# One projection piece of the fourth group moves from the eighth to the ninth step of the first attention branch, and the group's evacuation from the ninth to the tenth

## The reference, cut to what matters

```python
h = rmsnorm(x)
a_q, a_k, a_v, b_q, b_k, b_v, c_q, c_k, c_v, c_f, gates = split(h @ w_in)
# A, 4 heads, two maps each of width 64, values of width 128, keys up to the query's chunk of 64:
p = softmax(q k / 8 + t5 bias);  o_a = (p[map 0] - lam * p[map 1]) @ v, then a norm
# B, 8 heads: a band of 9 chunks; C, 8 heads: causal with a forget bias
x = x + (g0 * (o_a @ w_br_a) + g1 * (o_b @ w_br_b) + g2 * (o_c @ w_br_c)) @ w_out
x = x + (silu(h2 @ w_gate) * (h2 @ w_up)) @ w_down
out = rmsnorm(x)
```

## Time and profile before

| | us |
|---|---|
| median of 3 runs | 1947.63 |
| lowest, highest | 1944.6, 1948.3 |
| the profiled execution's own time | 1945.05 |
| its span | 1943.0 |
| PE busy | 1884.4 (97%) |
| DVE busy | 1150.8 (59%) |
| ACT busy | 815.8 (42%) |
| mean granted PE clock | 0.991 |

### The profile page before, as it was taken

The page is one execution under the profiler, slowest core; times in us unless marked ns, Lnnn a source line. Parts: engine busy times, 40 slices in busy tenths (PEclk is TensorE's granted clock), DMA queues, the critical chain, the costliest instruction groups (busy, mean ns, idle before and its releaser), DMA issues. The chain is left out here.

```text
span 1943.0 us, 27344 instructions
## 1 busy us (share of the span) xinstructions
PE 1884.4 (97%) x9286; PEld 1580.8 (81%) x9286; DVE 1150.8 (59%) x2167; ACT 815.8 (42%) x1519; POOL 252.1 (13%) x259
## 2 busy tenths in 40 slices
PE   6999999999999998999999999999999999999997
PEld 3888888888888887888888887777888888888886
DVE  5466766656676777224332237698567665676655
ACT  5556556666776666224331121443223322233223
POOL 2311111111111100000000000012121221212211
PEclk9999999999999999999999999999999999999998
DMA  8422222222222212213112122102111211112112
GB/s 239 127 72 76 66 78 68 80 58 65 81 61 80 79 44 83 59 48 92 42 45 71 49 83 102 48 22 66 58 50 43 65 43 57 51 43 65 43 44 98
DMA packets 145232, 133.24 MB, mean 69 GB/s; under 512 B 7316, under 2 KB 130324, under 8 KB 142856
## 3 DMA queue, kind: packets, MB, share of 16 engines
q1 hardware_dynamic: 142936, 131.77, 22.8%
q10 hardware_dynamic: 2224, 0.56, 0.1%
HBM read 109.17 MB, written 16.06 MB: 64 GB/s over the span
## 5 line engine op out<-in xcount | busy, mean ns | idle before, releaser
L196 PE MATMUL ps<-h_hi,w_hi 128*128 128x512 f32 x1104 | 446.1, 404 | 6.2 <-DVE h_lo L2011 2.9
L198 PE MATMUL ps<-h_hi,w_lo 128*128 128x512 f32 x1104 | 433.0, 392 | 0.0
L197 PE MATMUL ps<-h_lo,w_hi 128*128 128x512 f32 x1104 | 432.1, 391 | 0.0
L196 PEld LDWEIGHTS ps<-h_hi,w_hi 128*128 128x128 f32 x1104 | 208.6, 189 | 47.9 <-DVE h_lo L2011 3.6
L198 PEld LDWEIGHTS ps<-h_hi,w_lo 128*128 128x128 f32 x1104 | 208.3, 189 | 45.9
L197 PEld LDWEIGHTS ps<-h_lo,w_hi 128*128 128x128 f32 x1104 | 208.6, 189 | 37.8
L1980 DVE TENSOR_TENSOR residual<-residual,ps 128x512 f32<-128x512 f32 x240 | 162.3, 685 | 118.1 <-PE ps L198 109.8
L752 POOL TENSOR_TENSOR w_lo<-w_raw,w_hi 128x256 fp32r<-128x256 f32 x138 | 102.0, 770 | 550.6 <-ACT w_hi L779 515.4
L1881 ACT ACTIVATE w_hi<-bias 128x512 fp32r<-128x512 f32 x60 | 38.0, 633 | 295.5 <-POOL bias L1764 220.4
L1764 POOL TENSOR_TENSOR bias<-w_raw 128x512 f32<-128x512 f32 x20 | 26.1, 1304 | 997.3 <-DVE act_lo L1994 573.6
L196 PE MATMUL ps<-w_down_hi,act_hi 128*128 128x512 f32 x352 | 137.0, 389 | 0.3 <-issue 0.3
(11 more groups left out here) (287 smaller groups left out, 3835.1 us busy)
## 6 DMA issues: line engine op xcount, KB each, us to landing
w_raw<-in_w_in SPq DMA_DIRECT2D x60, 512.0 KB, 3.8
w_raw<-in_w_gate_up SPq DMA_DIRECT2D x44, 512.0 KB, 3.7
k_stack<-k_stack SPq DMA_DIRECT2D x24, 512.0 KB, 5.5
w_down_raw<-in_w_down SPq DMA_DIRECT2D x11, 1024.0 KB, 4.9
x_all<-in_x SPq DMA_DIRECT2D x8, 512.0 KB, 8.5
bias<-bias_a_scratch SPq DMA_DIRECT2D x4, 1024.0 KB, 6.0
heads_bc_scratch<-heads_out SPq DMA_DIRECT2D x8, 512.0 KB, 2.9
bias<-neg_c_scratch SPq DMA_DIRECT2D x4, 1024.0 KB, 5.1
```

The lines of the kernel that those rows point to most:

```text
L196: nc.tensor.matmul(out, w_hi, x_hi, start=first, stop=False)
L197: nc.tensor.matmul(out, w_hi, x_lo, start=False, stop=False)
L198: return nc.tensor.matmul(out, w_lo, x_hi, start=False, stop=last)
```

## The change

In the table for branch A one piece is taken from s = 7 and given to s = 8, and the evacuation of group 3 goes from s = 8 to s = 9, on ACT and on DVE. Branches B and C, the last unit and every other group keep their steps. No instruction is added or removed.

```diff
 PIECES_AT = [
-    [2, 2, 2, 2, 1, 1, 1, 1, 0, 0, 2, 1, 1, 1, 1, 2, 0],
+    [2, 2, 2, 2, 1, 1, 1, 0, 1, 0, 2, 1, 1, 1, 1, 2, 0],
...
 EVAC_AT = [
-    {0: 0, 2: 1, 4: 2, 8: 3, 13: 4, 16: 5},
+    {0: 0, 2: 1, 4: 2, 9: 3, 13: 4, 16: 5},
```

## The result

| | before | changed |
|---|---|---|
| median us (6 runs each) | 1947.16 | 1953.9 |
| lowest, highest us | 1942.78, 1948.3 | 1952.52, 1954.75 |
| span of the profiled execution, us | 1943.0 | 1951.1 |
| mean granted PE clock in it | 0.991 | 0.994 |

Changed to before: 1.004, with a 95% interval of 1.0028 to 1.0051. The change makes the kernel 6.7 us slower by the medians.

The account below looks back on a forecast made before the run. PE, busy 97% of the span, was taken to bound the kernel. Stall 7 plus clock 5 made 12 us: 1957 on the profiled 1945.05, 1959.6 on the median; forecast between them, 1958, range 1952 to 1963.

Parts of the forecast that it names:

- The stall: Branch A, first piece of step 10: PE waits longer for line 925 in four units, 7 us net, none hidden.
- The earlier `mix_maps`: Branch A: scores of step 10 are ready earlier, `mix_maps` ends 0.70 us earlier in the first unit; 3.3 us gained in all.
- the wait that goes is the whole effect: Rival: PE's `mix_maps` wait shrinks and the evacuation lands in time; 1942 us, 1944 on the median; chance 0.04.
- ACT: Step 9: evacuation behind `exp(10)`, ahead of `o_low` and `chunks_hi`, uses up the head start; `chunks_hi` still starts at 109.50.
- DVE: Step 9: evacuation stands behind `read_scores(11)` and both `chunks_low`, which wait for ACT; line 925 ends at 112.19, not 110.28.
- No recovery in the unit: Behind the moved piece on PE's queue: no wait of PE in the rest of the unit can absorb the delay.
- The clock: PE's new gaps of 2.5 to 2.8 us lower its clock in three of four units: 5.1 us, bounds 0 and 6.8.
- the first rival: The stall without the clock, none or one of four gaps makes it fall: 1952 to 1954, up to 1956; chance 0.2.
- The forecast case: Branch A: the stall and two to four clock falls, 1955.5 to 1961.5 us; chance 0.65.

Follow-up runs that it names:

- The piece alone: Against the kernel before, only the piece moves from s = 7 to s = 8, the evacuation stays at s = 8; 1942.39 us, ratio 0.9978.
- the low part ahead of `chunks_low`: The whole change, but in step 9 DVE does the evacuation's low part before `chunks_low`, not behind it; 1946.88 us, ratio 1.0004 to the kernel before.
- the eight profiles with both edits: The whole change profiled twice, and once each with 2, 4, 6, 8, 10 and 12 extra matmuls ahead of the attention; 1951.93 to 1955.69 us.
- the evacuation alone: Against the kernel before, only the evacuation of group 3 moves from s = 8 to s = 9, the piece stays at s = 7; 1959.48 us, ratio 1.0067.
- 6 extra matmuls: The whole change plus 6 matmuls on PE ahead of the attention's first pieces, their sums overwritten; 1955.06 us in one run.
- the evacuation at step 10: The whole change with the evacuation one step later, at s = 10 on ACT and DVE; 1970.19 us, ratio 1.0118 to the kernel before.

## Why the prediction was right, and where it was not

**The stall (right).** Forecast 7 us, 5.9 to 7.9; the waits give 6.5, the start of branch B 6.53, and 6.7 is measured. Its parts, in the first unit: DVE was to read the scores of step 10 at 105.89 and did at 105.82; line 925 was to end at 112.19 and ended at 111.37 + 0.69 = 112.06; the piece was to start at 112.25 and started at 112.11. The forecast total of waits, "below 2" for line 1001 and "about 10" for line 925, came out as 1.8 and 11.1.

**The earlier `mix_maps` (right, a little small).** 3.3 us forecast, 3.7 by the waits. In the first unit 0.07 of the rest is DVE's: the forecast let it start when the record of line 1012 ends, 105.89, and it started at 105.82. The piece alone isolates the gain: 3.9 us faster. The mechanism of the rival "the wait that goes is the whole effect" is thus real, and it decides once the evacuation stays at its step.

**ACT (nearly right).** "No later and no earlier" for `chunks_hi`: it started at 109.23 and not at 109.50. `exp` of step 10 came 0.08 before its forecast, and two ACT instructions began about 0.1 us before the record ahead of them ended: line 793 behind `exp`, and `chunks_hi` behind `o_low` (108.96 + 0.37 against 109.23). Half of that 0.27 reaches line 925, which ended 0.13 before its forecast.

**DVE (right, and shown).** With the low part ahead of `chunks_low` 5.8 of the 6.5 us of waits are gone.

**No recovery in the unit (right).** The 6.5 us at the end of the branch are the sum of the four units' stalls.

**The clock (wrong).** "With two of three falling, three of the four units are likely to fall: 3 x 1.7 = 5.1 us". None fell in the profile of the change, and two in the 32 gaps of the eight profiles with both edits. This term is the whole error of the point forecast: 1945.05 + 7 is 1952, and 1954.6 from the first median, where 1953.9 was measured. The price per fall, 1.7 us, was a little high: 1.5 with the evacuation alone and with 6 extra matmuls. The chance was far off: I read it from three gaps in other stages and treated four gaps of one loop as if each drew for itself. The case that held was the first rival, the stall with none or one fall, "1952 to 1954 on the profiled time", to which I gave 0.2. The forecast case by itself, 1955.5 to 1961.5, missed; that 1953.9 lies in the range 1952 to 1963 is owed to its having been drawn over this rival. The sentence that the trace disagrees with the Trainium skill, "TensorE: Matmul & The Clock Gate", section "HAM oscillation — how this bites in real kernels", claims too much as well. Its rule that gaps this short leave the clock alone gave 1952. It is not strictly true, since four gaps of 2.40 us did bring it down, but for this change it was the better guide.

## What to carry to other kernels

When work is moved one step in an in-order schedule, take its parts one by one: here the producer's move gained 3.9 us and the consumer's move lost 10.2, and the two waits in the profile, with the clock's falls, added up to the measured medians within half a microsecond, to one of them (the evacuation at step 10) partly by chance. Before delaying an evacuation, look for what it will stand behind on each engine, above all an instruction that waits for a third engine. If the bank's next user already waits for it, however little (0.22 us here), expect every bit of further delay to be paid in full, as it was here.

## What the runs showed of the hardware

A fall of the granted clock to 1.2 GHz behind these gaps cost PE about 1.5 us by the times of the work behind it (1.7 by the mean clock of a window); one of four lasted twice as long where the gap was 4.6 us, 3.3 us by its window. PE gaps of 2.40 us had a fall behind them in 4 of 36 cases, gaps of 4.6 us in 4 of 4, gaps of 1.0 us in none of 4, and gaps of equal length in units with the same work of one execution differed. The mean clock of a whole execution, 0.994 in the changed kernel and 0.991 before, says nothing of a stage: the change adds gaps, and the number went up, as two of the falls elsewhere happened to be half as long.
